# Six of sixteen key pages per sequence scored by GpSimd products and VectorE sums instead of TensorE

## The chip, the core and the metric

The kernel runs on one core of a Trainium2 chip. The metric is the device time of one execution in microseconds, as the median of the runs shown. The core has a matrix engine (TensorE, in the rows PE, with PEld for its weight loads), three element-wise engines (VectorE, DVE; ScalarE, ACT; GpSimd, POOL), and a queue engine, SyncE, whose rows read SP or SPq. Each engine runs its own instruction list in order; semaphores order them against each other.

## What is computed

One layer of a decoder: a prompt of 512 tokens and eight sequences of four new tokens each. The change touches only the stick-breaking attention of the eight sequences over their 2048 cached keys, which lie in 16 pages of 128 keys:

```
k_past = cache_k_sb[page_table]                     # 8 sequences x 16 pages x 128 keys x 8 heads x 64
z_past = einsum('bthd,bkhd->bhtk', q, k_past)       # 4 queries, 8 heads: 32 scores for each key
z      = concat([z_past, z_new]) * 64**-0.5 + bias
w      = stick_breaking_weights(z, mask)            # needs all scores: log terms, then sums over later keys
o      = einsum('bhtk,bkhd->bthd', w, v_past) + einsum('bhtk,bkhd->bthd', w_new, v_new)
```

Beside it the same sequences attend, in eight other heads, to a dilated window of 896 rows of another buffer (the window work below).

## The kernel before

A program of stages: projections, prompt attention, the *sample stage* (366 to 875 us of the span), output projection and feed-forward, experts. The sample stage alone is changed, and one small transfer is added in the projections.

The sample stage is written out by hand as nine *turns*, 0 to 8. In turn b the keys of sequence b are scored while the values of sequence b - 1 are weighed; so turn 0 has no values and turn 8 no keys. Turns 1 to 6 are one hardware loop. A turn has 16 *steps*, 0 to 15, and every engine's list is written step by step (functions `turn`).

- **Keys, one page a step.** SP loads a page (256 KB) into one of 8 slots, half a turn ahead. PE transposes it (line 991, four transposes into PSUM), ScalarE copies the result to SBUF (L1160), and in the next step PE scores it (`score`, L1001: four products of a 128x128 weight and 8 columns). When all 16 are scored, VectorE's `logits` (L1261) scales and biases them.
- **The chain on the scores, at the start of the next turn.** ScalarE forms log terms (L1171 to L1173), VectorE sums them up (L1309 to L1317), PE sums over keys in step 3 (`sums`, L1009 and L1010), VectorE subtracts (L1324), ScalarE takes exponents, and VectorE splits the weights (L1327, step 4).
- **Values, two pages a step from step 7.** SP loads into 4 slots; a slot is free again when VectorE has subtracted. ScalarE copies the high part (L1184), VectorE subtracts to get the low part (L1331, two SBUF operands), PE weighs (`weigh`, L1023), one step later.
- **The window work.** PE scores in steps 0 and 1 (L1055); VectorE takes the maximum and the sum's inputs in step 2 (`window_logits`, to L1234); PE turns the weights in step 5 (L1064); VectorE copies them (`copy_turned`, L1244 and L1245); PE weighs the window in steps 6 to 8 (L1073). From step 9 PE turns the next sequence's window keys through one PSUM bank (L1043), which ScalarE (L1147) and VectorE (L1270) empty by turns.
- **SP's list.** In each step: the key load, which waits for the slot; the value loads; the window loads in steps 1 and 10. It runs in order, so a load that waits holds all behind it.
- **GpSimd** copies the window queries once a turn (L1126) and issues five 4 MB copies of the window state, one each in turns 0 to 4 (L570, in the order of turns).

Of the kernel before, what the change touches and what calls it, by code (L numbers as in the profile page):

```python
# [25 lines left out]
F32 = mybir.dt.float32  # L26
# [8 lines left out]
P = 128  # L35
# [39 lines left out]
NW = NEAR + FAR  # L75
K_SLOTS = 8
ALL_COLUMNS = 52992
# [88 lines left out]
def build(nc, x_prompt, x_sample, cache_k_sb, cache_v_sb, page_table, state_k_win, state_v_win,  # L166
# [4 lines left out]
    with ExitStack() as ctx:  # L171
        kept = ctx.enter_context(nc.sbuf_tensor("kept", [P, KEPT], F32))
        pages_sb = ctx.enter_context(nc.sbuf_tensor("pages_sb", [1, DB * PAGES], I32))
        psum = ctx.enter_context(nc.psum_tensor("psum", [P, 8 * BANK], F32))
        gates_dram = nc.dram_tensor("gates_dram", [NCHUNK, P, NK * CHUNK], F32).ap()
        gelu_dram = nc.dram_tensor("gelu_dram", [SETS, P, ND], F32).ap()

        made = {}
        AGAIN = {"early_in_0": "dl_out_scaled", "early_in_1": "dl_scores", "early_turned": "dl_turn",
                 "early_copied": "dl_turned", "early_hidden": "o_t_copied", "early_gelu": "o_t_ready",  # L180
# [9 lines left out]
                 "v_rows_in_4": "sb_softplus", "gates_in_0": "sb_sums", "gates_in_1": "dl_exp"}  # L190

        def sem(name):
            name = AGAIN.get(name, name)
# [138 lines left out]
        @part("pool")  # L332
        def _(pool):

            def rows_out(tile, prompt, sample, name, ready, value):
                pool.wait_ge(sem(ready), value)
                pool.dma_start(prompt, tile[:, 0:4, :]).then_inc(sem(f"{name}_out"), 16)
                if name in ("k_sb", "v_sb"):
                    pool.dma_start(sample, tile[0:NS, 4, :]).then_inc(sem(f"{name}_out"), 16)
                else:  # L340
                    for b in range(DB):
                        pool.dma_start(sample[b], tile[b * DT:(b + 1) * DT, 4, :])\
                            .then_inc(sem(f"{name}_out"), 16)
# [12 lines left out]
            pool.wait_ge(sem("k_dil_out"), (1 + DB) * 16)  # L356
# [58 lines left out]
        def _(act):  # L415
# [31 lines left out]
            for c in range(len(GROUPS)):  # L447
                if c in (2, 3):
                    act.wait_ge(sem("qk_ready"), 5 * (c - 1))
                if c == 3:  # L450
# [395 lines left out]

        k_page = [take(DH) for _ in range(K_SLOTS)]
        v_page = [take(DH) for _ in range(V_SLOTS)]
        ss_e = take(SW)
# [54 lines left out]
        def _(sp):  # L904
# [18 lines left out]

            def load(b, j, cache, to, free, name):
                g = PAGES * b + j
                page = sp.value_load(pages_sb[0:1, bass.ds(g, 1)], min_val=0, max_val=N_POOL - 1)  # L926
                sp.wait_ge(sem(free), g + 1)
                sp.dma_start(to[j % len(to)], cache[bass.ds(page, 1)].rearrange("o p c -> (o p) c"))\
                    .then_inc(sem(f"{name}_{j % len(to)}"), 16)

            def keys(b, j):
                load(b, j, cache_k, k_page, "page_turned", "k_page")

            def values(b, j):
                load(b, j, cache_v, v_page, "page_v_low", "v_page")

            def turn(b, pages, before):

                for s in range(PAGES):
                    if s < PAGES - K_SLOTS and pages:  # L940
                        keys(b, K_SLOTS + s)
                    if s >= PAGES - K_SLOTS and pages and not (isinstance(b, int) and b == DB - 1):
                        keys(b + 1, s - (PAGES - K_SLOTS))
                    if before:
# [15 lines left out]
            for j in range(K_SLOTS):  # L960
                keys(0, j)
            window_values(0)
            turn(0, True, False)
# [6 lines left out]
        def _(pe):  # L970
# [16 lines left out]
            def turn_page(b, j):  # L987
                pe.wait_ge(sem(f"k_page_{j % K_SLOTS}"), 32 * b + 16 * (j // K_SLOTS) + 16)
                pe.wait_ge(sem("page_copied"), PAGES * b + j + 1)
                for pair in range(NPAIR):  # L990
# [4 lines left out]
            def score(b, j):  # L995
                if j == 0:
                    pe.wait_ge(sem("seq_logits"), 2 * b + 1)
                pe.wait_ge(sem("page_copied"), PAGES * b + j + 3)
                for pair in range(NPAIR):
# [90 lines left out]
            def turn(b, pages, before):  # L1090
                for s in range(PAGES):
                    if pages:
                        turn_page(b, s)
                        if s >= 1:
                            score(b, s - 1)
                        if s == 0:
# [16 lines left out]
                if before:  # L1113
                    weigh(b - 1, PAGES)
                if pages:
                    score(b, PAGES - 1)
                if before:
# [4 lines left out]
        @part("pool")  # L1122
        def _(pool):
            for b in range(DB):
                pool.wait_ge(sem("dw_scores"), b + 1)
                pool.tensor_copy(q_b, q_wide[:, :, b:b + 1, :].rearrange("p c o n -> p (c o) n"))\  # L1126
                    .then_inc(sem("q_b_ready"), 1)
                if b >= 1 and 3 + b < len(MOVES):
                    move_state(pool, 3 + b)

        @part("act")
        def _(act):
# [22 lines left out]
            def turn(b, pages, before):  # L1155
                for s in range(PAGES):
                    if pages:
                        act.wait_ge(sem("page_scored"), PAGES * b + s + 1)
                        act.wait_ge(sem("page_turned"), PAGES * b + s + 1 + K_SLOTS)
                        act.activation(k_turned[s % 2], bank(s % 2).rearrange("p (c n) -> p c n", c=NPAIR), ACT.Copy)\  # L1160
                            .then_inc(sem("page_copied"), 1)
                        if s == EXP_W_AT:
# [6 lines left out]
                    if s == 0:  # L1169
                        act.wait_ge(sem("seq_logits"), 2 * b + 1)  # L1170
                        st.link(act.activation(ss_e, ss_z[:, 0:SW], ACT.Abs))  # L1171
# [17 lines left out]
        def _(dve):  # L1189
# [69 lines left out]
            def logits(b):  # L1259
                dve.wait_ge(sem("page_scored"), PAGES * b + PAGES + 2)  # L1260
                dve.scalar_tensor_tensor(ss_z[:, 0:SW].rearrange("p (j n) -> p j n", j=PAGES),  # L1261
                                         bank(2).rearrange("p (j n) -> p j n", j=PAGES), SCALE,
                                         flat_bias.rearrange("p (o n) -> p o n", o=1).to_broadcast([P, PAGES, HT]),
                                         ALU.mult, ALU.add).then_inc(sem("seq_logits"), 1)
# [8 lines left out]
            for m in range(1, NW, 2):  # L1273
# [20 lines left out]
            def turn(b, pages, before):  # L1294
                for s in range(PAGES):
                    if pages and s in (TOP_AT, NORM_AT, KEYS_AT):
                        window_step(b, s)
                    if before:
                        page_step(b, s)
                    if pages and s not in (TOP_AT, NORM_AT, KEYS_AT):  # L1300
                        window_step(b, s)
                close(b, pages, before)

            def page_step(b, s):
                if True:
                    if s == 0:
                        dve.wait_ge(sem("seq_log"), b)
                        dve.wait_ge(sem("seq_logits"), 2 * b + 1)
                        st.do(dve.scalar_tensor_tensor(ss_p[:, 0:SW], ss_z[:, 0:SW], 0.0, ss_e, ALU.max, ALU.add))  # L1309
# [1056 lines left out]
```

## Time and profile before

| | |
|---|---|
| median of 3 runs | 2478.3 us (2473.87 to 2479.03) |
| the profiled execution | 2474.16 us, span 2472.3 us |
| TensorE busy | 2304.7 us (93%) |
| VectorE, ScalarE, GpSimd busy | 1549.5, 942.2, 393.3 us |
| sample stage, turns 0 to 7 | 388.3 to 838.4 us of the span |
| granted TensorE clock, whole span | 0.958 of full speed |

A busy PE is not PE at its peak: matmuls are pipelined and their ends are modelled. In a timeline row the first number is the start from the span's start, the second the length of the merged piece; the bracket gives the idle time before it and what ended it.

### The profile page before, as it was taken

Reading aid. Unit: us, or ns where it says so; the run is one execution under the profiler, and the core shown is the slowest. Engines: PE = TensorE matmul, PEld = TensorE weight load, DVE = VectorE, ACT = ScalarE, POOL = GpSimd, SP = SyncE. Lnnn points to the kernel's source line nnn. Section 1 sums busy time; section 2 is a strip of 40 time slices with the busy share of each in tenths; the row PEclk is TensorE's granted clock in tenths of the full one; section 3 lists DMA queues with packets and bytes.
Section 4 is the critical chain, followed back from the end, with each engine's and each line's share of the span. In section 5 each row is a group of like instructions: output and inputs, shape, how many; then the busy total and the mean of one; then the engine's idle time right before and its main releaser. Section 6 shows DMA issues by size and latency. Waiting matters only on the chain.

```text
span 2472.3 us, 37860 instructions
## 1 busy us (share of the span) xinstructions
PE 2304.7 (93%) x12921; PEld 1901.2 (77%) x12921; DVE 1549.5 (63%) x3167; ACT 942.2 (38%) x1432; POOL 393.3 (16%) x370
## 2 busy tenths in 40 slices
PE   7998988998999798999899889999999999999996
PEld 7997765666566446985577688999989899999895
DVE  4352331333444434678998778777777777777777
ACT  3225542444444512223355633333333333333332
POOL 0001000000000000000000044333333333333320
PEclk9999987889999898999999999999999999999998
DMA  4226977877766621203254699999999999999982
GB/s 130 87 88 224 332 237 271 275 263 263 267 207 209 196 66 37 83 21 106 92 197 178 243 333 342 317 313 315 314 313 311 316 315 311 312 313 313 311 294 78
DMA packets 224111, 568.20 MB, mean 230 GB/s; under 512 B 18065, under 2 KB 96466, under 8 KB 221330
## 3 DMA queue, kind: packets, MB, share of 16 engines
q1 hardware_dynamic: 174994, 327.75, 40.2%
q0 software_dynamic: 49024, 239.23, 27.6%
q8 instruction: 56, 0.92, 0.1%
q14 instruction: 37, 0.30, 0.0%
HBM read 528.24 MB, written 105.12 MB: 256 GB/s over the span
## 4 chain that ended last, share of the span: by engine, by line
PE 79%; DVE 8%; DMA 4%; ACT 3%; SPq 3%; issue 2%; POOL 0%; ACTq 0%; DVEq 0%
PE psum L2065 20%; PE psum L2056 16%; PE psum L405 7%; PE psum L1560 5%; PE psum L1839 5%; PE psum L2046 3%; DMA sample<-in_cache_v_sb_dram 3%; PE psum L1862 3%; PE psum L1420 3%; PE psum L1001 3%; PE psum L1055 2%; PE psum L991 2%; PE psum L1073 2%; PE psum L1023 1%; SPq L926 1%
## 5 line engine op out<-in xcount | busy, mean ns | idle before, releaser
L2065 PE MATMUL psum<-expert_parts 128*128 128x512 f32 x2304 | 550.3, 394 | 0.8 <-DVE expert_parts L2184 0.8
L2065 PEld LDWEIGHTS psum<-expert_parts 128*128 128x128 f32 x2304 | 426.7, 188 | 87.3 <-DVE expert_parts L2184 1.8
L2056 PE MATMUL psum<-h_parts,expert_parts 128*128 128x384 f32 x2304 | 444.5, 341 | 2.9 <-DVE expert_parts L2179 1.5
L2056 PEld LDWEIGHTS psum<-h_parts,expert_parts 128*128 128x128 f32 x2304 | 403.0, 189 | 10.9 <-issue 1.8
L2126 ACT ACTIVATE expert_parts<-peer 128x1024 fp32r<-128x1024 f32 x128 | 135.8, 1061 | 358.9 <-PE psum L2065 332.8
L2179 DVE TENSOR_TENSOR expert_parts<-psum,expert_parts 128x512 fp32r<-128x512 f32 x192 | 132.8, 692 | 147.2 <-ACT expert_parts L2120 147.2
L2222 DVE SCALAR_TENSOR_TENSOR kept<-experts,kept 128x1024 f32<-128x1024 f32 x160 | 205.0, 1281 | 8.3 <-DMA experts<-in_peer_v_dram,kept 3.0
L2031 POOL DMA_INDIRECT experts<-in_peer_v_dram,kept x160 | 192.6, 1204 | 70.5 <-issue 47.5
L1839 PE MATMUL psum<-h_whole,gate_table 128*128 128x384 f32 x512 | 180.6, 497 | 10.5 <-ACT gate_table L1891 10.5
L1331 DVE TENSOR_TENSOR sample_parts<-sample,sample_parts 128x512 fp32r<-128x512 f32 x128 | 85.5, 690 | 166.9 <-ACT sample_parts L1184 166.5
L405 PE MATMUL psum<-projection_parts 128*128 128x256 f32 (+1 forms) x1440 | 174.5, 283 | 3.8 <-DVE projection_parts L511 3.8
L405 PEld LDWEIGHTS psum<-projection_parts 128*128 128x128 f32 (+1 forms) x1440 | 170.6, 175 | 6.0 <-issue 3.9
L2120 ACT ACTIVATE expert_parts<-psum 128x512 fp32r<-128x512 f32 x192 | 114.8, 598 | 149.1 <-PE psum L2046 142.5
L2184 DVE TENSOR_TENSOR expert_parts<-peer,expert_parts 128x1024 fp32r<-128x1024 f32 x128 | 155.9, 1218 | 0.0
L1839 PEld LDWEIGHTS psum<-h_whole,gate_table 128*128 128x128 f32 x512 | 93.8, 193 | 67.5 <-issue 18.1
L2026 POOL DMA_INDIRECT experts<-in_peer_u_dram,kept x96 | 95.3, 992 | 314.4 <-DVE experts L2206 180.2
L1160 ACT ACTIVATE sample<-psum 128x512 f32<-128x512 f32 x128 | 75.8, 593 | 164.4 <-PE psum L991 164.4
L2026 POOL DMA_INDIRECT peer<-in_peer_u_dram,kept x62 | 79.7, 1285 | 361.9 <-DVE peer L2206 356.6
L1001 PEld LDWEIGHTS psum<-attention,sample 128*128 128x128 f32 x1024 | 134.7, 204 | 1.6 <-issue 0.8
L2046 PE MATMUL psum<-kept,peer 128*128 128x128 f32 x768 | 115.7, 273 | 16.1 <-DVE expert_parts L2179 15.7
L1001 PE MATMUL psum<-attention,sample 128*128 (+1 forms) x1024 | 130.5, 254 | 0.0
L1023 PE MATMUL psum<-sample_parts 128*64 128x512 f32 x272 | 96.4, 482 | 25.0 <-DVE sample_parts L1331 24.2
(281 smaller groups left out, 3287.1 us busy)
## 6 DMA issues: line engine op xcount, KB each, us to landing
peer<-in_peer_v_dram SPq DMA_DIRECT2D x128, 512.0 KB, 5.0
peer<-in_peer_u_dram SPq DMA_DIRECT2D x96, 512.0 KB, 5.4
sample<-in_cache_k_sb_dram SPq DMA_DIRECT2D x128, 256.0 KB, 3.9
sample<-in_cache_v_sb_dram SPq DMA_DIRECT2D x128, 256.0 KB, 3.0
out_dram<-in_state_k_win_dram POOLq DMA_DIRECT2D x8, 4088.0 KB, 54.4
out_dram<-in_state_v_win_dram POOLq DMA_DIRECT2D x8, 4088.0 KB, 41.2
gates_dram<-gate_table SPq DMA_DIRECT2D x12, 2048.0 KB, 7.3
experts<-gates_dram SPq DMA_DIRECT2D x32, 768.0 KB, 6.8
```

What stands on the lines that cost most here:

```text
L405: last = pe.matmul(bank(u % 4)[0:r, 0:WC], lhsT=x_r[:, x, k, t * P:t * P + r], rhs=w_in_r[g % 2][:, y, k, :], start=(n == 1), stop=(n == 3 ...
L1001: last = pe.matmul(bank(2)[:, c:c + 8].rearrange("p (e t) -> p e t", e=2), lhsT=k_turned[j % 2][:, pair, :], rhs=q_s["sb"][:, 2 * pair:2 * ...
L1839: last = pe.matmul(bank(6)[:, 0:ND], lhsT=early_t[e % 2][:, k, :], rhs=h1_f[:, k, :], start=(k == 0), stop=(k == KD - 1))
L2026: pool.indirect_dma_start(out=u_rows[p], out_offset=None, in_=peer_u, in_offset=index(q, p))\
L2031: pool.indirect_dma_start(out=v_rows[p], out_offset=None, in_=peer_v, in_offset=index(q - 1, p))\
L2046: last = pe.transpose(bank(7)[:, k % 4 * P:(k % 4 + 1) * P], u_sb[s][:, k * P:(k + 1) * P], ident)
L2056: last = pe.matmul(bank(6)[:, 0:ND], lhsT=u_t[s][:, a, k, :], rhs=h1_r[:, b, k, 0:ND], start=(k == 0 and n == 0), stop=(k == KD - 1 and n ...
L2065: last = pe.matmul(bank(2 * t + half), lhsT=weight[s][:, a, t * P:(t + 1) * P], rhs=v_r[s][:, b, half * 512:(half + 1) * 512], start=(firs ...
L2126: act.activation(v_r[s][:, 0, :], v_sb[s], ACT.Copy).then_inc(sem("v_high"), 1)
L2179: dve.tensor_tensor(u_t[s][:, 1, ks, :], bank(7).rearrange("p (k j) -> p k j", k=4), u_t[s][:, 0, ks, :], ALU.subtract).then_inc(sem("u_lo ...
L2184: dve.tensor_tensor(v_r[s][:, 1, :], v_sb[s], v_r[s][:, 0, :], ALU.subtract).then_inc(sem("v_low"), 1)
L2222: dve.scalar_tensor_tensor(y, v_rows[p], dots_act[:, p:p + 1], y, ALU.mult, ALU.add).then_inc(sem("added"), 1)
```

## The change

Of each sequence's 16 pages PE now scores ten (`TURNED`); the other six (`DOTTED`) are scored without it. Each sequence's four query rows are written to DRAM in the projections and broadcast from there to all 128 partitions (1 MB each, on GpSimd's queue, one turn ahead). GpSimd multiplies a key page with two query rows at a time, so two products of 128x1024 a page, into two buffers; VectorE sums each product over the 64 elements of a head (`page_dot`). PE has a page in steps 0, 1, 2, 3, 5, 6, 8, 10, 12, 14. VectorE sums in steps 2, 4, 7, 9, 12, 14. The eight slots are split into five and three. `logits` becomes one instruction for the six pages and one for the ten.

```diff
-K_SLOTS = 8
+K_SLOTS = 5
+P_SLOTS = 3
+TURNED = 10
+DOTTED = PAGES - TURNED
...
+        PAGE_STEPS = (0, 1, 2, 3, 5, 6, 8, 10, 12, 14)
+        DOT_STEPS = (2, 4, 7, 9, 12, 14)
+        P_LOAD_STEPS = (3, 5, 8, 10, 13, 15)
...
+            pool.wait_ge(sem("proj_copied"), 10)
+            pool.dma_start(q_rows_dram, staged[0][0:NS, 4, :]).then_inc(sem("q_rows_out"), 16)
...
+                    if s in P_LOAD_STEPS and pages:
+                        i = P_LOAD_STEPS.index(s)
+                        if i + P_SLOTS < DOTTED or more(b):
+                            sp.wait_ge(sem("page_product"), 2 * DOTTED * b + 2 * i + 2)
...
-                        turn_page(b, s)
-                        if s >= 1:
-                            score(b, s - 1)
+                        if s in PAGE_STEPS:
+                            j = PAGE_STEPS.index(s)
+                            turn_page(b, j)
+                            if j >= 1:
+                                score(b, j - 1)
+                        if s == PAGES - 1:
+                            score(b, TURNED - 1)
...
+            for b in range(DB):
+                if b + 1 < DB:
+                    if b >= 1:
+                        pool.wait_ge(sem("page_product"), 2 * DOTTED * b)
+                    query_rows(b + 1)
                 if b >= 1 and 3 + b < len(MOVES):
                     move_state(pool, 3 + b)
...
+                for i in range(DOTTED):
+                    pool.wait_ge(sem(f"p_page_{i % P_SLOTS}"), 16 * DOTTED // P_SLOTS * b + 16 * (i // P_SLOTS) + 16)
+                    for e in range(2):
+                        n = 2 * DOTTED * b + 2 * i + e
+                        if n >= 2:
+                            pool.wait_ge(sem("page_reduced"), n - 1)
+                        pool.tensor_tensor(products[e], q_rows[b % 2][:, 2 * e:2 * e + 2, :],
+                                           p_page[i % P_SLOTS].rearrange("p (o c) -> p o c", o=1).to_broadcast([P, 2, DH]),
+                                           ALU.mult).then_inc(sem("page_product"), 1)
+                    if i == 1 and b + 1 < DB:
+                        window_queries(b + 1)
...
+            def page_dot(b, i):
+                for e in range(2):
+                    n = 2 * DOTTED * b + 2 * i + e
+                    dve.wait_ge(sem("page_product"), n + 1)
+                    dve.tensor_reduce(page_dots[:, i * HT:(i + 1) * HT].rearrange("p (h t) -> p t h", t=DT)[:, 2 * e:2 * e + 2, :],
+                                      products[e].rearrange("p t (h d) -> p t h d", d=HD), AX_X, ALU.add)\
+                        .then_inc(sem("page_reduced"), 1)
...
                     if before:
                         page_step(b, s)
+                    if pages and s in DOT_STEPS:
+                        page_dot(b, DOT_STEPS.index(s))
                     if pages and s not in (TOP_AT, NORM_AT, KEYS_AT):
                         window_step(b, s)
```

VectorE's list before, in steps 4 to 7 of a looped turn (`normalise` L1240, weights L1327, `copy_turned` L1244 and L1245, first value page L1331; ISA and REGISTER_ALU rows set up waits):

```order
L1240 TENSOR_SCALAR sample<-sample,kept 32x928
L1327 TENSOR_TENSOR sample_parts<-sample,sample_parts 128x17x32
L1244 COPY sample<-psum 128x224
L1245 COPY sample<-psum 32x32
L1330 ISA
L1331 TENSOR_TENSOR sample_parts<-sample,sample_parts 128x512
```

The same place now, where L1355 is `page_dot`, L1311 and L1312 are `copy_turned`, and L1412 is a value page:

```order
L1307 TENSOR_SCALAR sample<-sample,kept 32x928
L1408 TENSOR_TENSOR sample_parts<-sample,sample_parts 128x17x32
L1354 REGISTER_ALU
L1355 TENSOR_REDUCE sample<-attention 128x2x8
L1354 REGISTER_ALU
L1355 TENSOR_REDUCE sample<-attention 128x2x8
L1311 COPY sample<-psum 128x224
L1312 COPY sample<-psum 32x32
L1411 ISA
L1412 TENSOR_TENSOR sample_parts<-sample,sample_parts 128x512
```

The two sums of the second page now stand ahead of `copy_turned`. VectorE's list before at the end of a turn, step 14 and the closing (two value pages, the copy of a turned window key tile, the copy of the weighed values):

```order
L1331 TENSOR_TENSOR sample_parts<-sample,sample_parts 128x512
L1330 REGISTER_ALU
L1331 TENSOR_TENSOR sample_parts<-sample,sample_parts 128x512
L1269 REGISTER_ALU
L1270 COPY w_out_sb<-psum 128x4x128
L1337 COPY sample<-psum 64x512
```

And now, with the same four instructions at L1412, L1412, L1341 and L1418:

```order
L1412 TENSOR_TENSOR sample_parts<-sample,sample_parts 128x512
L1411 REGISTER_ALU
L1412 TENSOR_TENSOR sample_parts<-sample,sample_parts 128x512
L1354 REGISTER_ALU
L1355 TENSOR_REDUCE sample<-attention 128x2x8
L1354 REGISTER_ALU
L1355 TENSOR_REDUCE sample<-attention 128x2x8
L1340 REGISTER_ALU
L1341 COPY w_out_sb<-psum 128x4x128
L1418 COPY sample<-psum 64x512
```

The sums of the sixth page stand between the last values and the window key copy that PE's last step waits for.

## Rows read from the trace of the kernel before

**Rows 1.** Windows, turns 0, 1, 4, 7: busy us per engine, PEclk, DMA share, GB/s

```profile
388.30:434.20 45.90, 45.90 (x274) 32.67 (x272) 6.47 (x18) 14.12 (x24) 0.73 (x2) 0.85 0.75 260
434.20:496.40 62.20, 58.24 (x317) 40.62 (x316) 23.45 (x48) 27.46 (x45) 0.73 (x2) 0.86 0.80 265
618.70:676.70 58.00, 51.91 (x315) 35.48 (x314) 23.64 (x50) 27.45 (x45) 0.73 (x2) 0.97 0.83 280
792.00:838.40 46.40, 46.13 (x285) 31.02 (x284) 21.21 (x47) 24.62 (x41) 0.00 (x0) 1.00 0.75 248
```

**Rows 2.** Chain that ended last, by line, turn 4

```profile
by line: DMA sample<-in_cache_v_sb_dram 24.9%; PE psum L1055 11.2%; PE psum L1001 9.6%; PE psum L991 7.3%; issue 6.4%; PE psum L1023 5.8%; SPq L926 5.0%; PE psum L1073 4.6%; ACT sample_parts L1184 4.4%; SPq L928 4.4%; DVE sample_parts L1331
```

**Rows 3.** Timeline of PE, turn 4, steps 2 to 8: start us, us, what

```profile
627.18 0.66 PE L991 MATMUL psum<-kept,sample 128*128 128x128 f32 x4
...
628.48 0.64 PE L991 MATMUL psum<-kept,sample 128*128 128x128 f32 x4
...
636.33 2.76 PE L1073 MATMUL psum<-sample 128*32 128x512 f32 x6
639.02 0.66 PE L991 MATMUL psum<-kept,sample 128*128 128x128 f32 x4
...
640.41 2.76 PE L1073 MATMUL psum<-sample 128*32 128x512 f32 x6
643.10 0.66 PE L991 MATMUL psum<-kept,sample 128*128 128x128 f32 x4
```

**Rows 4.** Timeline of VectorE, turn 4, steps 2 to 6

```profile
629.12 0.14 DVE L1234 TENSOR_SCALAR kept<-kept 32x1 f32<-32x1 f32 x1
631.77 0.69 DVE L1324 TENSOR_TENSOR sample<-sample,psum 128x512 f32<-128x512 f32 x1 [2.51 <-PE psum L1010]
...
634.04 0.72 DVE L1327 TENSOR_TENSOR sample_parts<-sample,sample_parts 128x544 fp32r<-128x544 f32 x1 [0.80 <-ACT sample_parts L1179]
...
635.52 0.17 DVE L1245 COPY sample<-psum 32x32 f32<-32x32 f32 x1
```

**Rows 5.** Lines by form: VectorE reductions, GpSimd's copy

```profile
L1687 DVE TENSOR_REDUCE kept<-kept 128x8 f32<-128x128 f32 x4 | 1.1, 282 | 6.0 <-ACT kept L1896 6.0
...
L1687 DVE TENSOR_REDUCE kept<-kept 128x2 f32<-128x32 f32 x1 | 0.2, 186 | 7.2 <-ACT kept L1896 7.2
...
L1126 POOL COPY sample<-attention 128x128 f32<-128x128 f32 x8 | 2.3, 292 | 522.4 <-PE psum L1055 372.3 <-PEq L978 150.0
```

**Rows 6.** Timeline of the SP queue, turn 4: value loads of steps 7, 9, 12

```profile
641.72 3.29 SPq L928 DMA_DIRECT2D sample<-in_cache_v_sb_dram  x2
...
653.10 1.55 SPq L928 DMA_DIRECT2D sample<-in_cache_v_sb_dram  x2
...
666.95 1.55 SPq L928 DMA_DIRECT2D sample<-in_cache_v_sb_dram  x2
```

**Rows 7.** Timeline of ScalarE, turn 4: what value page 4 waits for

```profile
651.58 1.35 ACT L1184 ACTIVATE sample_parts<-sample 128x512 fp32r<-128x512 f32 x2 [1.78 <-DMA sample<-in_cache_v_sb_dram]
```

**Rows 8.** Timeline of VectorE, turn 4, steps 14 and 15

```profile
671.90 0.69 DVE L1331 TENSOR_TENSOR sample_parts<-sample,sample_parts 128x512 fp32r<-128x512 f32 x1 [0.53 <-ACT sample_parts L1184]
672.51 0.68 DVE L1270 COPY w_out_sb<-psum 128x512 f32<-128x512 f32 x1
```

**Rows 9.** Timeline of PE, turn 4, step 15

```profile
673.25 0.66 PE L1043 MATMUL psum<-kept,w_out_sb 128*128 128x128 f32 x4 [0.37 <-DVE w_out_sb L1270]
```

**Rows 10.** Timeline of PE, turn 0, step 6

```profile
409.19 4.42 PE L1073 MATMUL psum<-sample 128*32 128x512 f32 x6
```

**Rows 11.** Timeline of PE, turn 6, step 12

```profile
777.86 1.11 PE L1043 MATMUL psum<-kept,w_out_sb 128*128 128x128 f32 x4 [2.03 <-DVE w_out_sb L1270]
```

**Rows 12.** Timeline of VectorE, turn 0, step 2

```profile
400.42 0.14 DVE L1234 TENSOR_SCALAR kept<-kept 32x1 f32<-32x1 f32 x1
```

**Rows 13.** Start of the stage: PE's first wait

```profile
375.36 1.11 PE L1043 MATMUL psum<-kept,w_out_sb 128*128 128x128 f32 x4 [7.90 <-DMA w_out_sb<-in_state_k_win_dram]
```

**Rows 14.** Windows: the 5 us before that

```profile
370.00:375.00 5.00, 0.00 (x0) 0.00 (x0) 1.60 (x4) 2.53 (x4) 0.00 (x0) 0.50 1.02 385
```

More of the change, by code:

```diff
@@ L449, in _ @@
                     act.wait_ge(sem("qk_ready"), 5 * (c - 1))
+                if c == 2:
+                    act.wait_ge(sem("q_rows_out"), 16)
                 if c == 3:
@@ L847, in build @@
         k_page = [take(DH) for _ in range(K_SLOTS)]
+        p_page = [take(DH) for _ in range(P_SLOTS)]
+        q_rows = [take(DT * DH).rearrange("p (t c) -> p t c", t=DT), v_n["dil"][:, 0:DT, :]]
+        products = [v_n["sb"][:, 2 * e:2 * e + 2, :] for e in range(2)]
+        page_dots = take(DOTTED * HT)
+        PAGE_STEPS = (0, 1, 2, 3, 5, 6, 8, 10, 12, 14)
+        DOT_STEPS = (2, 4, 7, 9, 12, 14)
+        P_LOAD_STEPS = (3, 5, 8, 10, 13, 15)
         v_page = [take(DH) for _ in range(V_SLOTS)]
@@ L922, in window_values, with page_at @@
                 window(b, 1, vw, "vw_in")
[L924 to L929, printed above, removed]
-            def keys(b, j):
-                load(b, j, cache_k, k_page, "page_turned", "k_page")
+            def page_at(b, j):
+                return sp.value_load(pages_sb[0:1, bass.ds(PAGES * b + j, 1)], min_val=0, max_val=N_POOL - 1)
@@ new lines, in load, with dot_keys @@
+            def load(page, cache, to, signal):
+                sp.dma_start(to, cache[bass.ds(page, 1)].rearrange("o p c -> (o p) c")).then_inc(sem(signal), 16)
+            def keys(b, j):
+                page = page_at(b, j)
+                sp.wait_ge(sem("page_turned"), TURNED * b + j + 1)
+                load(page, cache_k, k_page[j % K_SLOTS], f"k_page_{j % K_SLOTS}")
+            def dot_keys(b, i):
+                load(page_at(b, TURNED + i), cache_k, p_page[i % P_SLOTS], f"p_page_{i % P_SLOTS}")
@@ L934, in values @@
             def values(b, j):
-                load(b, j, cache_v, v_page, "page_v_low", "v_page")
+                page = page_at(b, j)
+                sp.wait_ge(sem("page_v_low"), PAGES * b + j + 1)
+                load(page, cache_v, v_page[j % V_SLOTS], f"v_page_{j % V_SLOTS}")
             def turn(b, pages, before):
                 for s in range(PAGES):
[L940 to L943, printed above, removed]
+                    if s in PAGE_STEPS and pages:
+                        j = PAGE_STEPS.index(s) + K_SLOTS
+                        if j < TURNED:
+                            keys(b, j)
+                        elif more(b):
+                            keys(b + 1, j - TURNED)
+                    if s in P_LOAD_STEPS and pages:
+                        i = P_LOAD_STEPS.index(s)
+                        if i + P_SLOTS < DOTTED or more(b):
+                            sp.wait_ge(sem("page_product"), 2 * DOTTED * b + 2 * i + 2)
+                            if i + P_SLOTS < DOTTED:
+                                dot_keys(b, i + P_SLOTS)
+                            else:
+                                dot_keys(b + 1, i + P_SLOTS - DOTTED)
@@ L961, in _ @@
                 keys(0, j)
+            for i in range(P_SLOTS):
+                dot_keys(0, i)
             window_values(0)
@@ L1123, in _, with query_rows, window_queries @@
         def _(pool):
-            for b in range(DB):
+            def query_rows(b):
+                rows = q_rows_dram[b * DT:(b + 1) * DT, :].rearrange("t c -> (t c)").rearrange("(o n) -> o n", o=1)
+                pool.dma_start(q_rows[b % 2].rearrange("p t c -> p (t c)"), rows.to_broadcast([P, DT * DH]))\
+                    .then_inc(sem(f"q_rows_in_{b % 2}"), 16)
+            def window_queries(b):
                 pool.wait_ge(sem("dw_scores"), b + 1)
@@ L1127, in _ @@
                     .then_inc(sem("q_b_ready"), 1)
+            pool.wait_ge(sem("q_rows_out"), 16)
+            query_rows(0)
+            window_queries(0)
+            for b in range(DB):
[3 more added lines that the diff above has]
+                    query_rows(b + 1)
                 if b >= 1 and 3 + b < len(MOVES):
                     move_state(pool, 3 + b)
+                rows_in = f"q_rows_in_{b % 2}"
+                pool.wait_ge(sem(rows_in), ON_FROM[rows_in][1] + 16 * (b // 2) + 16)
+                for i in range(DOTTED):
[9 more added lines that the diff above has]
+                        window_queries(b + 1)
         @part("act")
@@ L1157, in turn @@
                     if pages:
[L1158 to L1161, printed above, removed]
+                        if s in PAGE_STEPS:
+                            j = PAGE_STEPS.index(s)
+                            act.wait_ge(sem("page_scored"), TURNED * b + j + 1)
+                            act.wait_ge(sem("page_turned"), TURNED * b + j + 1 + K_SLOTS)
+                            act.activation(k_turned[j % 2], bank(j % 2).rearrange("p (c n) -> p c n", c=NPAIR), ACT.Copy)\
+                                .then_inc(sem("page_copied"), 1)
                         if s == EXP_W_AT:
```

31 lines of the change are left out of this document (18 added, 13 removed).

## The prediction

> **What bounds the kernel now.** I read the windows of the turns first, then the chain of waits in one turn, then the timelines of PE, VectorE and the SP queue in that turn. Turns 0 and 7 are PE's own: busy 45.90 of 45.90 us and 46.13 of 46.40 [rows 1]. A full turn takes 62.2 us (turn 1, while state copies run) or 58.0 (turn 4), and PE is idle for 4 to 6 of them. In turn 4 the largest share of the chain, 24.9%, is a value page's transfer, ahead of any line of PE [rows 2]. So a full turn has two halves. In steps 0 to 8 PE runs without a gap. From step 9 the values set the pace: SP loads a page, it lands, ScalarE copies it, VectorE subtracts, which frees the slot for the next load. In that half SP issues one page load each 1.22 us (the two loads of step 9 take 1.55 together, 0.33 of it the second issue) [rows 6].
>
> **What is removed.** A page costs PE 1.30 us: step 2 begins at 627.18 and step 3 at 628.48, and the stretch holds one transposed and one scored page [rows 3]. Six pages in eight turns are 6 x 1.30 x 8 = 62 us. The six steps without a page are 4, 7, 9, 11, 13 and 15; five of them lie at step 7 or later, where the full turn is mostly not PE's.
>
> **What is added, unit prices.** A sum over 64 of a product of 1024 elements has no row. Reductions of 32 and of 128 elements take 186 and 282 ns [rows 5], so 1.0 ns an element, and 1024 take 282 + 896 x 1.0 = 1.18 us; two a page, 2.36. A GpSimd product has no row either. Its copy of 128 elements takes 292 ns [rows 5]; eight times that is 2.34 us, which I take. The lower bound is VectorE's rate, 1.2 us; the upper is one more pass of reads, 4.7. [...]
>
> **Steps 2 to 8 of a full turn: nothing gained.** VectorE is free at 629.26 and next needed at 631.77 [rows 4], so the first page's sums (2.36) just fit. The second page's products start when the first sum is done (630.4) and take 4.7, to 635.1. VectorE splits the weights at 634.04 to 634.76 [rows 4], then come the second page's sums, to 637.1, and only behind them `copy_turned`, about 0.5 long, which ended at 635.69 [rows 4]: now 637.6. PE's window weighing waits for it, so it starts near 637.8 instead of 636.33 [rows 3]. Behind it step 7 no longer has its page: the second piece begins at 640.5 (before 640.41), step 8 at 643.2 (before 643.10). The pages of steps 4 and 7 become a wait of PE of about 2.3 us. Term: 0.
>
> **Steps 9 to 15 of a full turn: what the loads give, the last sums take.** From the loads of step 9 (653.10) to the last value load (666.95 + 1.22 = 668.17) SP issues ten more page loads and four window loads [rows 6]; the new list has ten there too (fewer key loads, one for a product page). So only the start of step 9's loads can move. It waits for value page 4 to be subtracted. Page 4 was issued at 641.72 and reached ScalarE at 651.58 [rows 6, 7]; step 7 of ScalarE and VectorE no longer waits for PE, so its issue moves up by some 3 us, at most 3.2 in the end. At least it gains one page of PE, 1.1 to 1.3, since ScalarE's copy of the first window key in step 9 stands ahead of it. I take 2.2. At the end the sixth page's sums stand in VectorE's queue: today the last value page is subtracted at 671.90, the key copy follows at once (672.51), and PE's last step starts with it at 673.25 [rows 8, 9]. Now 2.36 us lie between. -2.2 + 2.4: term 0 for each of the six turns, from -3.2 (sums hidden) to +1.3.
>
> **The two PE turns.** In turn 0 VectorE is free at 400.56 [rows 12]. From there GpSimd's chain runs: sums 1.2, five page pairs 23.4, last sums 2.4, and one stop of about 3.5 because the fourth page's sums stand behind `window_rows`, which waits for PE's step 8; then the copy of the last window key and PE's last pieces, 1.1. That ends at 432 against 434.2 [rows 1]: -2, from -4 (product of 1.2) to +8 (of 4.7, 5 x 2 x 2.4 later, less what PE lets go). Turn 7 has no window keys; there values at 1.22 us a load and the same chain end about 2 us earlier: -2.
>
> **The start.** PE waits 7.90 us for the first window keys [rows 13], and in the last 5 us of that the DMA engines are full (1.02 of their time, 385 GB/s) [rows 14]. The query rows of sequences 0 and 1, 1.05 MB each, are now issued in the same moment: 2.1 MB at 385 GB/s is 5.4 us. 0 to +5.4; I take +4, since they share the engines until the keys are in. In later turns 1 MB more, and the state copies, issued after the last product instead of in step 2, go where value loads do not run: 0.
>
> **The clock.** Before the window weighing PE now has only transposes, 8-column products and a gap of 2.3 us. In turn 0, which has no `sums` there, the same six matmuls took 4.42 us instead of 2.76 [rows 3, 10]: the 1.2 GHz level. Behind a gap of 2.03 us in turn 6 four transposes took 1.11 instead of 0.66 [rows 9, 11], the same level. Nothing waits in SBUF there to hide it, so it costs 1.7 us in a turn where it happens; I take three of seven: +5 (0 to +12).
>
> **VectorE beside GpSimd.** No row shows the two at work together: GpSimd has 0.73 us in turn 4 [rows 1]. If a subtraction of two SBUF tiles cannot run beside a product, the split at 634.04 waits for the product that runs until 635.1, +1.1, and a value pair behind the sums of step 9 as much again: 0 to +2.3 a turn. I take +0.6, seven times: +4.
>
> **Sum.** -2 + 0 - 2 + 4 + 5 + 4 = +9 on the profiled execution's 2474.2: 2483. That execution lies 4.1 us below the median of its three runs, so on their scale 2487 us, 0.4% slower. What a measurement of this kernel can tell from no change is about 0.2%, 5 us.
>
> **A rule that speaks against the change.** GpSimd's 0.73 us in a turn [rows 1] leave the question above open. The Trainium skill (SBUF — State Buffer, Who interferes with whom) says that a VectorE instruction with two SBUF inputs and a GpSimd instruction that reads SBUF exclude each other for a whole instruction, and that `tensor_reduce` never contends. By that rule the term is 16 instead of 4; no run shows it yet.
>
> **Rivals.**
> 1. *Faster: the value loop moves up and the sums find gaps.* If VectorE's sums in step 14 end before the last value page lands and nothing blocks, each full turn gains 2.2 to 3.2 us: 6 x -2.7 - 4 - 2 + 2 = -20, 2458. For it: VectorE is busy only 23.64 of 58 us. Against: its list is in order, and the sixth sums stand behind the last values. It decides if the last sums start before the last values are subtracted.
> 2. *PE's pages all count:* -62, 2416. For it: 93% busy. Against: the chain of turn 4.
> 3. *VectorE and GpSimd exclude each other:* 16 for 4, and the products wait too: 2499.
> 4. *Products of 3.2 us or more.* Step 6 waits 0.8 us longer in seven turns and turn 0 becomes GpSimd's, +8 instead of -2: 9 + 6 + 10 = +25, 2503. At 4.7 a turn needs 56 us of GpSimd alone; then 2520. For it: two inputs instead of one.
>
> **How the numbers follow.** Forecast (2475 to 2492): 0.40. Rival 1: 0.25. Rival 2: 0.05. Rival 3: 0.18. Rival 4: 0.12. Faster than 2473.3: rivals 1 and 2 and little of the forecast, 0.33. Within 0.2%: somewhat under half of the forecast, 0.18. Slower: 0.49. The range leaves out rival 2, the far end of rival 1 and that of rival 4: 2450 to 2512. The likeliest case's own range is 2475 to 2492.
>
> **What would show it.** Right: PE's window weighing waits for VectorE's copy in step 6 of full turns; the last value load some 2 us earlier in the turn; PE's last step behind the sums; turns 1 to 6 within 1 us of before; the start of turn 0 some 4 us later; GpSimd's products near 2.3 us. Wrong: turns of 55 us (rival 1); subtractions longer than 0.69 us or late beside products (rival 3); products over 3 us (rival 4).

## The result, and the profile after

The changed kernel takes 2525.2 us (median of 4 runs, 2521.3 to 2527.8), the kernel before on the same occasion 2476.5. The ratio is 1.0197, 95% interval 1.0171 to 1.0223: 49 us slower. The forecast was 2487 with a range to 2512. The sign was right, the size was not. The profiled execution of after has a span of 2519.4 us, 47.1 more than that of before.

Windows of turns 0, 1, 4 and 7 of the kernel after, columns as in [rows 1]:

```profile
392.95:436.90 43.95, 38.24 (x204) 26.80 (x203) 23.65 (x31) 10.49 (x18) 28.17 (x15) 0.85 0.59 192
436.90:501.45 64.55, 50.41 (x241) 30.41 (x239) 47.42 (x61) 23.72 (x40) 32.55 (x16) 0.82 0.88 305
632.25:695.95 63.70, 49.70 (x243) 30.69 (x243) 46.13 (x62) 23.35 (x39) 31.15 (x15) 0.84 0.77 265
826.25:884.40 58.15, 48.97 (x212) 28.31 (x210) 44.70 (x58) 21.52 (x35) 25.08 (x10) 0.78 0.61 199
```

Counted from one first product of window scores to the next (turn 7 to the turning of its weighed values), turns 0 to 7 are longer by -1.9, 2.4, 4.5, 4.0, 5.6, 7.0, 8.1 and 12.4 us; the start takes 4.7 more, and what follows turn 7 takes 0.4 more. PE is busy in turn 4 for 49.7 of 63.7 us, VectorE for 46.1, about twice as long as before. The chain of turn 4, by line; no value page's transfer leads it any more [rows 2]:

```profile
by line: issue 16.3%; PE psum L1109 15.3%; PE psum L1091 10.2%; DVE sample L1355 10.1%; DVE sample_parts L1412 9.2%; PE psum L1059 8.1%; PE psum L1027 5.4%; PE psum L1037 5.0%; PE psum L1079 4.5%; DVE w_out_sb L1341 3.0%; ACT sample_parts L
```

The lines by form, kernel after (busy us, mean ns of one | idle before): the value subtraction, the products, the sums, the split of the weights, and the scaling of the window's weights.

```profile
L1412 DVE TENSOR_TENSOR sample_parts<-sample,sample_parts 128x512 fp32r<-128x512 f32 x128 | 142.2, 1152 | 72.7 <-ACT sample_parts L1251 72.7
L1190 POOL TENSOR_TENSOR attention<-attention,sample 128x1024 f32<-128x1024 f32 x48 | 117.6, 2471 | 127.9 <-DVE sample L1355 127.9
L1355 DVE TENSOR_REDUCE sample<-attention 128x16 f32<-128x1024 f32 x96 | 112.6, 1210 | 5.4 <-POOL attention L1190 5.4
L1408 DVE TENSOR_TENSOR sample_parts<-sample,sample_parts 128x544 fp32r<-128x544 f32 x8 | 17.4, 2174 | 4.4 <-ACT sample_parts L1246 4.4
L1307 DVE TENSOR_SCALAR sample<-sample,kept 32x928 f32<-32x928 f32 x8 | 7.8, 980 | 0.3
```

Both unit prices of the forecast hold: 2.47 us for a product, 2.36 in the median (2.34 forecast), 1.21 for a sum (1.18). But the same subtraction that took 690 ns now takes 1152 in the mean, and the split of the weights 2174 ns instead of 0.72 us [rows 4]. The mean hides two groups: 41 of the 128 subtractions take 0.95 to 2.85 us, and each of them runs while a product does; the others keep 0.69. Three groups of rows show how. GpSimd, VectorE and PE in turn 4, kernel after (start us, us):

```profile
644.16 5.09 POOL L1190 TENSOR_TENSOR attention<-sample 128x1024 f32<-128x1024 f32 x2 [13.74 <-DVE sample L1355]
647.41 2.42 DVE L1408 TENSOR_TENSOR sample_parts<-sample,sample_parts 128x544 fp32r<-128x544 f32 x1 [0.39 <-ACT sample_parts L1246]
...
651.11 5.09 POOL L1190 TENSOR_TENSOR attention<-sample 128x1024 f32<-128x1024 f32 x2 [1.13 <-DVE sample L1355]
652.40 4.34 DVE L1412 TENSOR_TENSOR sample_parts<-sample,sample_parts 128x512 fp32r<-128x512 f32 x2
652.61 7.89 PE L1109 MATMUL psum<-sample 128*32 128x512 f32 x12 [3.22 <-DVE sample L1312]
...
667.62 2.34 DVE L1355 TENSOR_REDUCE sample<-attention 128x16 f32<-128x1024 f32 x2
668.98 5.09 POOL L1190 TENSOR_TENSOR attention<-sample 128x1024 f32<-128x1024 f32 x2 [6.30 <-DVE sample L1355]
669.87 4.74 DVE L1412 TENSOR_TENSOR sample_parts<-sample,sample_parts 128x512 fp32r<-128x512 f32 x2
674.53 0.68 DVE L1341 COPY w_out_sb<-psum 128x512 f32<-128x512 f32 x1
675.27 1.12 PE L1079 MATMUL psum<-kept,w_out_sb 128*128 128x128 f32 x4 [6.03 <-DVE w_out_sb L1341]
```

Read from below: PE stands still for 6.03 us until VectorE has copied a turned window key. The copy itself takes 0.68, but ahead of it in VectorE's list stand the sums of step 9 (2.34) and a pair of value subtractions, and that pair takes 4.74 us instead of some 1.3 while the two products (5.09 instead of 4.7) run. So PE waits for VectorE, VectorE for GpSimd's products, and GpSimd, before that, had waited 6.30 us for one of VectorE's sums. The waits of PE in turns 0 to 8 (us in total, times, longest) show how often: in the kernel after

```profile
PE psum L1079 <- DVE w_out_sb L1341: 66.6, 18, 6.1
PE psum L1109 <- DVE sample L1312: 22.4, 7, 3.2
PE psum L1059 <- DVE sample_parts L1412: 13.4, 13, 3.6
```

and before, for the same three waits: 12.9 (L1270), none, 24.2 (L1331). PE never waits for a key page in these turns, and GpSimd once, before turn 0 (15.85 us), so the split of the eight slots into five and three is not what costs.

### The profile page after: what moved, and what is told of

Read it like the earlier page. It is cut to its first block, busy times and chain, and to the rows that moved or that the text cites. A ratio compares the mean times of both kernels' runs of the same rounds, so it can differ in the third digit from the quotient of the medians.

```text
span 2519.4 us, 36844 instructions
## 1 busy us (share of the span) xinstructions
PE 2267.8 (90%) x12345; PEld 1845.1 (73%) x12345; DVE 1731.4 (69%) x3271; ACT 912.0 (36%) x1384; POOL 637.1 (25%) x475
## 4 chain that ended last, share of the span: by engine, by line
PE 77%; DVE 13%; issue 4%; ACT 3%; DMA 2%; POOL 0%; SPq 0%; DVEq 0%; ACTq 0%; POOLq 0%
PE psum L2146 20%; PE psum L2137 16%; PE psum L414 7%; PE psum L1641 5%; PE psum L1920 4%; PE psum L2127 3%; PE psum L1943 3%; PE psum L1501 3%; PE psum L1109 3%; PE psum L1091 2%; DVE sample L1355 2%; DVE sample_parts L1412 2%; PE psum L1059 2%; PE psum L1079 1%; PE psum L1027 1%
## 5 line engine op out<-in xcount | busy, mean ns | idle before, releaser
L1412 DVE TENSOR_TENSOR sample_parts<-sample,sample_parts 128x512 fp32r<-128x512 f32 x128 | 142.2, 1152 | 72.7 <-ACT sample_parts L1251 72.7
L1190 POOL TENSOR_TENSOR attention<-sample 128x1024 f32<-128x1024 f32 x48 | 116.2, 2442 | 135.8 <-DVE sample L1355 119.9
L1190 POOL TENSOR_TENSOR attention<-attention,sample 128x1024 f32<-128x1024 f32 x48 | 117.6, 2471 | 127.9 <-DVE sample L1355 127.9
L1079 PE MATMUL psum<-kept,w_out_sb 128*128 128x128 f32 x224 | 45.4, 338 | 86.1 <-DVE w_out_sb L1341 68.2
```

What stands on the lines that cost most here:

```text
L1190: pool.tensor_tensor(products[e], q_rows[b % 2][:, 2 * e:2 * e + 2, :], p_page[i % P_SLOTS].rearrange("p (o c) -> p o c", o=1).to_broadcas ...
L1412: dve.tensor_tensor(v_parts[j % V_PARTS][:, 1], v_page[j % V_SLOTS], v_parts[j % V_PARTS][:, 0], ALU.subtract)\
```

## The experiments

Each was timed beside the kernel before on the same chip. Ratios are to it, with 95% intervals; "us" is the median.

**1. Products that read nothing.**

```diff
-  pool.tensor_tensor(products[e], q_rows[b % 2][:, 2 * e:2 * e + 2, :], p_page[...], ALU.mult)
+  pool.memset(q_rows[b % 2][:, 2 * e:2 * e + 2, :], 0.0)
+  pool.memset(products[e], 0.0)
```

> Each product on GpSimd is replaced by two fills of the same size that read nothing (one of the query rows, one of the product buffer); VectorE's 96 sums, their order and all waits stay. Theory A (a VectorE subtraction of two SBUF tiles and a GpSimd product that reads SBUF wait for one another): the value subtractions go back from a mean of 1152 ns to 690 to 750, the split of the weights from 2174 to 730, turn 7 from 58.2 us to under 52, and the time falls to 2485 to 2500. Theory B (VectorE's sums of 2.4 us a page stand in its queue ahead of what PE waits for): the time stays at 2510 or above, with PE still waiting some 68 us in all for VectorE's copies of the turned window keys.

Measured: 2492.8 us, ratio 1.0079 (1.0051 to 1.0108). Lines by form of this run:

```profile
L1411 DVE TENSOR_TENSOR sample_parts<-sample,sample_parts 128x512 fp32r<-128x512 f32 x128 | 84.6, 689 | 121.2 <-ACT sample_parts L1250 121.0
L1191 POOL MEMSET attention<- 128x1024 f32 x96 | 91.8, 956 | 0.0
L1306 DVE TENSOR_SCALAR sample<-sample,kept 32x928 f32<-32x928 f32 x8 | 17.1, 2143 | 0.3
```

The subtraction is back at 689 ns (36 of the 128 overlap a fill and take 0.68), the split of the weights is at 775, and the time lies in theory A's interval. Two fills take 1.9 us against 2.5 for a product, so a part of the 29 us between the two ratios may be that. On the other side the fills bring a delay of their own: the scaling of the window's weights takes 2143 ns, against 980 in the changed kernel. The profiled execution was the longest of its nine (2516.6), with turn 3 at 75 us, so its turns are not compared.

**2. Short sums.**

```diff
-  products[e].rearrange("p t (h d) -> p t h d", d=HD), AX_X, ALU.add)
+  products[e].rearrange("p t (h d) -> p t h d", d=HD)[:, :, :, 0:4], AX_X, ALU.add)
```

> The products stay; each sum takes 4 of the 64 columns of a head (64 elements instead of 1024, so some 0.2 us instead of 1.21). The rest of each dot product is left out. Theory B: VectorE's queue is shorter by 2 us a page, PE's waits for the copies of the turned window keys fall from 68 us to under 30, and the time comes to 2475 to 2495. Theory A: subtractions beside products stay at 1.1 us or more in the mean; the products follow one another without a pause, so more of a turn is covered by them early, and the time is 2500 or above.

Measured: 2488.6 us, 1.0059 (1.0038 to 1.0080). Lines by form of this run:

```profile
L1412 DVE TENSOR_TENSOR sample_parts<-sample,sample_parts 128x512 fp32r<-128x512 f32 x128 | 143.0, 1150 | 101.2 <-ACT sample_parts L1251 101.0
L1408 DVE TENSOR_TENSOR sample_parts<-sample,sample_parts 128x544 fp32r<-128x544 f32 x8 | 5.7, 708 | 1.4 <-ACT sample_parts L1246 1.4
```

The subtractions still take 1150 ns in the mean, as theory A says, and yet the time is theory B's; PE's waits for the key copies fell to 36 us, short of the 30 that B wanted. So neither theory is the whole: each cut alone takes away 60 to 70% of the loss. This cut is not of VectorE's list alone: the products move with the sums, and the split of the weights, which no longer meets one, is back at 708 ns. My added reason was wrong: the products do not follow one another without a pause, since each waits for a sum, and those stand in their steps; two pairs still start 46 and 54 us into turn 5.

**3. Nothing added.** Fills of one column for the products, and the short sums.

> Both are cut: GpSimd fills one column of each row in place of the product, and each sum takes 4 of 64 columns. What is left is PE without six pages, with the same waits. My reading of the turns (steps 9 to 15 belong to the loads of the values): a full turn gains at most 5 us, turns 0 and 7 up to 7, so 2425 to 2460. If PE's pages counted in full: 2416 or less. If the time stays at 2475 or above, what was added is not what makes the kernel slower.

Measured: 2517.8 us, 1.0179 (1.0141 to 1.0217). A miss, and a useful one. Turns 1 to 4 take 69 to 79 us. Timeline of turn 3 of this run:

```profile
622.86 0.51 POOL L581 DMA_DIRECT2D out_dram<-in_state_k_win_dram  x1
...
625.23 1.56 SPq L946 DMA_DIRECT2D sample<-in_cache_v_sb_dram  x2
...
641.81 0.63 ACT L1249 ACTIVATE sample_parts<-sample 128x512 fp32r<-128x512 f32 x1 [17.43 <-DMA sample<-in_cache_v_sb_dram]
```

GpSimd was done early, so its 4 MB state copy left 31 us before the turn's end, and a value page issued 2.4 us behind it landed 16.6 us after its issue; 3.0 us is the median. The copies' place follows GpSimd's work in the change, and had to be held fixed in the next runs.

**4. The sums behind VectorE's window copies.**

```diff
-  DOT_STEPS = (2, 4, 7, 9, 12, 14)     # page_dot ahead of window_step
+  DOT_STEPS = (2, 5, 7, 10, 12, 14)    # page_dot behind window_step
```

> Products and sums as in the changed kernel, but in each step VectorE's sums stand behind its copies for the window, and the second and the fourth page's sums move one step later (steps 5 and 10). Theory B: the copy of the turned weights and the copies of the turned window keys come 2.4 us earlier where a sum stood ahead of them; turns 1 to 6 get 2 to 4 us shorter each, and the time is 2500 to 2512. Theory A alone: the copies do not wait for a product, but the subtractions do, so the time stays within 5 us of 2525.

Measured: 2514.1 us, 1.0165 (1.0134 to 1.0196), just past B's range. By the ratios that is 8 us less than the changed kernel, and the two intervals overlap, so a gain is not shown. PE's waits for the key copies fell from 66.6 us to 15.1, but it now waits 41.7 for value subtractions (13.4 in the changed kernel) and 24.2 for the window rows (3.7). Another order mostly moves the wait.

**5 to 8. The changed kernel and runs 1 to 3 with the copies back in step 2** (edit shortened).

```diff
-  if b >= 1 and 3 + b < len(MOVES): move_state(pool, 3 + b)     # behind the last product
   ...  window_queries(b + 1)
+  if 4 + b < len(MOVES): move_state(pool, 4 + b)
```

> The changed kernel, but GpSimd issues each 4 MB state copy where it stood before, behind the copy of the window queries in step 2 of a turn, instead of behind the last product of the turn before. Theory C (in the run with neither products nor sums, a copy issued in mid-turn held a value page for 17 us; it is the copies' place that made that run slow, and in the changed kernel they come too late in a turn to hold anything): within 10 us of the changed kernel, 2512 to 2530. If the copies' place also costs the changed kernel: 2505 or less.

> One column filled in place of each product and sums over 4 of 64 columns, as before, and the copies back in step 2. Theory C: no value page waits 17 us any more, turns 1 to 4 fall from 69 to 79 us to 55 to 60, and the time is 2435 to 2465, which is what PE without six pages is worth. If the time stays at 2490 or above, fewer pages on PE make the kernel slower by something else, its granted clock first.

> Fills in place of the products (no reads on GpSimd), sums in full, copies back in step 2: VectorE's queue alone. In the earlier run of this kind turns 5 and 6, where no copies run, took 60.0 and 59.3 us, against 65.1 in the changed kernel and 57.6 before. From that: 2475 to 2490, the queue worth 2 us a turn. If the queue were the whole cost: 2510 or above.

> Products in full, sums over 4 of 64 columns, copies back in step 2: the waiting of subtractions and products for each other, without the queue. In the earlier run of this kind turns 5 and 6 took 58.4 and 57.5 us. From that: 2460 to 2480, since products that no sum holds up are done before the values are subtracted. If the exclusion alone were the cost: 2500 or above.

Measured:

| run | products | sums | us | ratio |
|---|---|---|---|---|
| 5 | full | full | 2538.8 | 1.0258 (1.0226 to 1.0290) |
| 7 | fills, no reads | full | 2513.9 | 1.0148 (1.0107 to 1.0188) |
| 8 | full | short | 2499.1 | 1.0108 (1.0077 to 1.0138) |
| 6 | tiny fills | short | 2483.6 | 1.0043 (1.0019 to 1.0068) |

Theory C fails twice. The later place of the copies is not neutral for the changed kernel: without it it loses another 0.6% of the time, so the change hides a gain there. And with nothing added and the copies back, PE without six pages is still no faster than before. The two runs with one cut missed as well, by 24 and 19 us: I had read their forecasts off turns 5 and 6 of runs 1 and 2. Each came out at about the time set for its own remaining cause alone (2510, 2500), and that cannot hold for both.

By the ratios, taking the reads away is worth 27 us, cutting the sums 37, both 53, each within 10 to 13 us by the intervals. That the two together are worth less than their sum (by 11) is inside that noise, but the trace has a place where either is enough to hold PE, its wait for the window weights (`copy_turned`). Waits of PE in run 5:

```profile
PE psum L1109 <- DVE sample L1312: 22.4, 7, 3.2
PE psum L1100 <- DVE sample L1307: 5.8, 8, 2.2
```

and in run 7:

```profile
PE psum L1109 <- DVE sample L1311: 5.9, 5, 1.3
PE psum L1100 <- DVE sample L1306: 15.1, 8, 3.4
```

In run 8 the first wait is gone. The second, for the scaled window weights, grows by 9 us with the reads away and by 8 with the sums cut (14.0), a price of the two edits themselves; so 27 and 37 may be too low.

Why six pages fewer bring nothing: the SP queue and ScalarE in turn 4 of run 6, which PE begins at 623.13:

```profile
642.01 1.57 SPq L946 DMA_DIRECT2D sample<-in_cache_v_sb_dram  x2
...
655.41 1.36 ACT L1249 ACTIVATE sample_parts<-sample 128x512 fp32r<-128x512 f32 x2 [4.75 <-DMA sample<-in_cache_v_sb_dram]
```

Value page 4 is issued 18.9 us into the turn, against 23.0 before (641.72 in [rows 6], the turn begins at 618.7 in [rows 1]). It is in use at 32.3, against 32.9 [rows 7]. Issued 4.1 us earlier, it comes 0.6 earlier. The state copy left at 634.54 in this turn, and from the issue to the use the DMA engines were busy for 0.90 of the time; that they, and not PE, held the page is the reading that fits both.

**9. Broadcasts of 16 columns.**

```diff
-  pool.dma_start(q_rows[b % 2].rearrange("p t c -> p (t c)"), rows.to_broadcast([P, DT * DH]))
+  pool.dma_start(q_rows[b % 2][:, 0, 0:16], rows[:, 0:16].to_broadcast([P, 16]))
```

> As the run with neither products nor sums and with the copies back in step 2, but each broadcast of query rows brings 16 columns of one row in place of 1 MB. Theory D (in turns with a state copy the DMA engines set when the first value pages of a turn land, some 32 us into it, whatever PE does, and 1 MB more of query rows makes such a turn 2.7 us longer at 385 GB/s): the start gives back 4 to 5 us and turns 1 to 4 get 2 to 4 us shorter each, so 2484 becomes 2460 to 2472. If the rows cost nothing: 2480 or above.

Measured: 2470.1 us, 0.9983 (0.9962 to 1.0005), 13.5 us below the run with full rows. Turns 1 to 5 are 1.6 to 3.3 us shorter each, theory D's size, though turn 5 has no copy. The start was not given back: PE's first wait is still 11.22 us, with broadcasts of 8 KB in place of 1 MB. So it is not their bytes alone that hold the window keys.

**10. The copies' place alone, in the kernel before** (edit shortened).

```diff
   if b >= 1 and 3 + b < len(MOVES):
+      pool.wait_ge(sem("page_v_low"), V_SLOTS + PAGES * (b - 1))   # b = 1: K_SLOTS + PAGES pages turned
       move_state(pool, 3 + b)
```

> The kernel before, with one part of the change alone: GpSimd issues each state copy at the end of a turn (in turn 0 when its last page is turned, in turns 1 to 4 when the last value page is subtracted) instead of in step 2. Putting the copies back made the changed kernel 13 us slower; so their new place should be a gain that the change hides: value pages 4 and 5 no longer wait 9.9 us behind a copy, turns 1 to 3 fall from 61 to 62 us to 58 to 59, and the time to 2462 to 2470. If the copies' place is nothing for the kernel before: 2472 to 2478.

Measured: 2468.7 us, 0.9964 (0.9936 to 0.9991): a small gain, in the range. The profiled execution (2481.5) was the longest of its ten and shows turns 1 to 4 at 61.3 to 61.7 us, so where the gain comes from is not shown.

**11. Four pages, early** (edit shortened; PE's pages are left out in steps 5 to 8, and VectorE's sums stand behind its window copies).

```diff
-  K_SLOTS, P_SLOTS, TURNED = 5, 3, 10;  DOT_STEPS = (2, 4, 7, 9, 12, 14)
+  K_SLOTS, P_SLOTS, TURNED = 6, 2, 12;  DOT_STEPS = (2, 5, 7, 8)
+  pool.wait_ge(sem("kw_in"), 64)                          # ahead of the first query rows
+  pool.wait_ge(sem("page_v_low"), V_SLOTS + PAGES * b)    # ahead of rows, copy, next products
```

> A full kernel made from the findings: four pages instead of six go to GpSimd and VectorE, PE leaves them out in steps 5 to 8; VectorE's sums stand in steps 2, 5, 7 and 8, behind its copies for the window; the next turn's first products, the next query rows and the copies wait until the last value page of a turn is subtracted; and the first rows are loaded behind the first window keys. If the exclusion and the queue cost what they do because products and sums reach into the steps of the values: the last key copies no longer wait for sums, turns of 56 to 59 us, 2455 to 2475. If products of steps 5 to 8 still hold the subtractions of pages 0 to 5 on the path: 2480 to 2500.

Measured: 2529.2 us, 1.0225 (1.0177 to 1.0273): a miss by 29 us even from the slower of its two ranges, and no faster than the change with six pages (1.0197; the intervals overlap). Timeline of its turn 5:

```profile
740.63 4.42 DVE L1425 TENSOR_TENSOR sample_parts<-sample,sample_parts 128x512 fp32r<-128x512 f32 x2
744.97 2.33 DVE L1368 TENSOR_REDUCE sample<-attention 128x16 f32<-128x1024 f32 x2
747.23 0.67 DVE L1329 COPY sample<-psum 32x512 f32<-32x512 f32 x1
748.04 1.09 PE L1079 MATMUL psum<-kept,w_out_sb 128*128 128x128 f32 x4 [9.12 <-DVE sample L1329]
```

The same sequence, now ahead of the copy of the window rows: PE waits for that copy seven times, 50.3 us in all. With a third fewer pages the time did not fall, which fits a cost set by what stands behind a sum or a held subtraction and not by the number of pages; this run alone does not show it.

**12. Two pages, early.** As 11, with `TURNED = 14`, `DOT_STEPS = (2, 5)`, PE's pages left out in steps 6 and 7.

> As the full kernel with four pages, but two: PE leaves out the pages of steps 6 and 7, VectorE's sums stand in steps 2 and 5, where it waits for PE otherwise, and no product runs from step 6 to the last value page. In the kernel with four pages the sums of step 8 stood ahead of VectorE's copy of the window rows, for which PE waited 9.1 us in one turn; here nothing stands there. By theory: PE saves 2.6 us in each turn, of which the split of the weights and the query rows take 1.5 to 2 back; with the copies late (2469 by themselves) 2455 to 2470. If the sums of step 5 or the products beside the split hold the path all the same: 2475 to 2490.

Measured: 2464.3 us, 0.9964 (0.9941 to 0.9987): in the forecast range, and 0.4% below the kernel before. Its subtraction takes 689 ns in the mean, since no product runs beside one; the split of the weights takes 1059. PE's first wait is 7.66 us. It is not told apart from run 10, the copies' place alone, so the two pages themselves bring nothing that these runs can show.

## Why the prediction was wrong

Two terms of the sum failed, both far too small: VectorE beside GpSimd (+4, where taking the reads away is worth 27 to 29 us) and the queue behind the sums in steps 9 to 15 (0, where cutting the sums is worth 37). What was right is that the pages taken from PE gain nothing in full turns: run 9, which has next to nothing in their place, is level with the kernel before, and rival 2 is out.

- **The start, +4:** the size was right, but the reason is not borne out, so that is luck in part. PE's first wait grew from 7.90 [rows 13] to 11.90 us, and with the rows issued behind the window keys (runs 11 and 12) it was 7.74 and 7.66. So the place of the rows costs it. But I priced their 2.1 MB, and with 16 KB (run 9) the wait is 11.22; what holds the window keys there stays open.
- **Turn 0, -2:** right (-1.9). The products' price was right, so rival 4 is out.
- **VectorE beside GpSimd, +4: the step that failed.** Taking the reads away is worth 27 us with the copies back and, by 1.0197 against 1.0079, 29 with them late. I allowed up to two waits of 1.1 us in a turn and took half of one. The rows show that a pair of subtractions waits for two products in succession (4.3 to 4.8 us for 1.3), and that there are 15 such pairs, two in each of seven turns and a third in turn 7, and 11 single ones. Together the 128 subtractions grew by 57 us, and the split by 1.7 us in seven turns. Rival 3 had the mechanism and, at 16, under two thirds of the size. The rule of the Trainium skill (SBUF — State Buffer, Who interferes with whom) is borne out: the subtraction of two SBUF tiles waits for a GpSimd instruction that reads SBUF (1152 ns in the mean) and not for one that only writes (689), and the reductions keep their 1.21 us in either case.
- **Steps 2 to 8, 0:** the order was as forecast, the size was not. PE's window weighing waits for `copy_turned`, but 3.22 us where I had 2.3: it begins 20.4 us into turn 4, forecast 19.1, before 17.6. The split takes 2.42 us there, because it meets a product of the second page; the sums follow only behind it.
- **Steps 9 to 15, -2.2 + 2.4:** wrong on both sides. I put the late sums ahead of PE's last step alone; the sums of step 9 stand ahead of a key copy as well, and PE lost 6.03 us there. Cutting the sums is worth 37 us; a part of that is the split of steps 2 to 8, which goes back to 0.71 us with them. And the earlier load gains little: [rows 7] already held the sign, 9.9 us from issue to use where 3.0 is the median, a page that waited for its transfer while PE was ahead.
- **Turn 7, -2:** wrong by the most, +12.4. I took its values at the loads' rate of 1.22 us. Without window keys the turn is values and sums: four subtractions in succession took 5.99 us beside two products, PE waited behind them, and the granted clock fell from 1.00 [rows 1] to 0.78. With products and sums both cut (run 6) the turn is indeed 2 us shorter than before.
- **The clock, +5 (0 to +12):** the window weighing's 112 matmuls over window rows are busy for 66.2 us instead of 54.2, so +12, the upper bound. In turn 4 the granted clock is 0.50, the 1.2 GHz level, from 652.6 to 657.1 us, behind PE's wait of 3.22 us. The lower level reaches further than that line: over turns 0 to 7 PE's busy time falls by 38.6 us (420.4 to 381.8, granted clock 0.92 to 0.85), not by the 62 of the six pages, so it takes an estimated 24 us of PE's time; how much of it other waits hide is not shown.
- **Later turns' rows and copies, 0:** wrong twice, in opposite directions. 1 MB of rows a turn costs 13.5 us in all (run 9, with the copies in step 2), and the copies' later place gives about as much back (run 5 against the change). Turn 4, which I set beside turn 1 as if no copy ran in it, holds the fifth one, issued at 627.55.

In a chain of runs: PE without six pages and rows of 16 columns, 0.9983; with the rows, 1.0043; with products and sums, 1.0258; with the copies late, 1.0197, which is the change. What stays open: the split of the 53 us for products and sums where both hold the same place, and which part of the first is the clock's.

## What to carry to other kernels

Work moved to GpSimd is not free beside VectorE's instructions with two SBUF inputs when it reads SBUF: here each such instruction waited for up to 2.2 us, nearly a whole product. Look for them in the time where the moved work will run, and count a wait for each one. In an in-order list ask not whether the engine has idle time, but who waits for what stands behind the new instruction. And read a load's time from issue to use before crediting an earlier issue.

## What the runs showed of the hardware

A `tensor_scalar` of one SBUF tile by a value per partition (32x928) took 691 ns in the kernel before, 980 in the changed kernel and 2143 beside fills that only write (run 1), although the two-input subtraction did not notice those. And a 256 KB load issued 2.4 us behind a 4 MB DRAM copy landed 16.6 us after its issue (run 3; the median is 3.0).
